# End of a row of gated tiles in a hybrid decoder trunk: the order of the last row, the next weights' split and the forms

## What is computed

```python
def swiglu(x, wi, wo):
    g, u = jnp.split(x @ wi, 2, axis=-1)
    return (jax.nn.silu(g) * u) @ wo

def ffn_half(x, g_pre, g_post, wi, wo):
    return x + 0.5 * rmsnorm(swiglu(rmsnorm(x, g_pre), wi, wo), g_post)
```

## Time and profile before

| what | value |
|---|---|
| time of the kernel, median of 3 runs (lowest to highest) | 2131.16 us (2128.97 to 2131.18) |
| time of the profiled execution itself | 2131.25 us |
| span of the profile, first to last instruction | 2129.5 us |
| TensorE busy | 2045.5 us, 96% |
| VectorE, ScalarE, GpSimd busy | 1385.2, 799.4, 299.6 us |
| mean granted TensorE clock | 0.986 of full speed |
| HBM traffic over the span | 93 GB/s |

### The profile page before, as it was taken

How to read it: one execution, slowest core, us unless ns; L and a number is a source line. 1 busy time by engine, 2 the same in 40 slices (tenths; PEclk the granted TensorE clock), 3 DMA queues, 4 the chain that set the end, 5 groups by cost and what they waited for, 6 DMA issues and landing times.

```text
span 2129.5 us, 38394 instructions
## 1 busy us (share of the span) xinstructions
PE 2045.5 (96%) x16696; PEld 2015.8 (95%) x16696; DVE 1385.2 (65%) x1963; ACT 799.4 (38%) x1053; POOL 299.6 (14%) x293
## 2 busy tenths in 40 slices
PE   8999899999999989899999999998998998999899
PEld 8899899999999989899999999998998998999898
DVE  6756365856768746456687656474987873746567
ACT  5423133423354413233444323232485441423243
POOL 1022040032200004032000031230000001303100
PEclk9999999999999999999999999999999999999999
DMA  4222232144422223223222222222222212323222
GB/s 162 82 88 86 87 105 100 65 155 152 157 72 80 77 77 108 87 90 116 94 80 79 92 94 95 92 85 80 87 95 80 100 68 76 106 90 100 100 90 80
DMA packets 69960, 202.83 MB, mean 95 GB/s; under 512 B 6144, under 2 KB 40224, under 8 KB 60320
## 3 DMA queue, kind: packets, MB, share of 16 engines
q1 hardware_dynamic: 64368, 183.88, 25.0%
q0 software_dynamic: 5424, 16.50, 2.4%
HBM read 193.78 MB, written 4.48 MB: 93 GB/s over the span
## 4 chain that ended last, share of the span: by engine, by line
PE 67%; DVE 17%; ACT 6%; DMA 6%; issue 4%; POOL 1%; DVEq 0%; ACTq 0%; SPq 0%
PE acc L2102 26%; PE acc L2283 14%; PE acc L2272 13%; PE acc L2212 9%; DMA raw<-in_weights 6%; DVE w_lo L1273 3%; ACT w_hi L824 3%; DVE t L1386 2%; PE acc L2143 1%; DVE x L1393 1%; DVE act_lo L1399 1%; DVE rs_post L1381 1%; DVE y L1554 1%; DVE form_lo L1573 1%; PE acc L2341 1%
## 5 line engine op out<-in xcount | busy, mean ns | idle before, releaser
L1273 DVE TENSOR_TENSOR w_lo<-raw,w_hi 128x1024 fp32r<-128x1024 f32 (+3 forms) x245 | 454.6, 1856 | 171.8 <-ACT w_hi L824 171.7
L824 ACT ACTIVATE w_hi<-raw 128x1024 fp32r<-128x1024 f32 (+3 forms) x245 | 373.7, 1546 | 415.7 <-DMA raw<-in_weights 273.4
L2283 PE MATMUL acc<-act_hi,w_hi 128*128 128x260 f32 x1056 | 298.6, 283 | 1.8 <-DVE act_lo L1573 1.8
L2283 PE MATMUL acc<-act_lo,w_hi 128*128 128x260 f32 x1056 | 298.2, 282 | 0.0
L2283 PE MATMUL acc<-act_hi,w_lo 128*128 128x260 f32 x1056 | 298.1, 282 | 0.0
L674 POOL TENSOR_TENSOR raw<-raw 128x512 f32<-128x512 f32 x66 | 124.4, 1884 | 1184.0 <-DMA raw<-in_weights 1184.0
L2102 PE MATMUL acc<-hid_hi,w_hi 128*128 128x260 f32 x1024 | 213.4, 290 | 48.4 <-DVE hid_lo L1626 47.0
L2102 PEld LDWEIGHTS acc<-hid_hi,w_hi 128*128 128x128 f32 x1024 | 163.2, 195 | 51.3 <-DVE hid_lo L1626 49.5
L2102 PE MATMUL acc<-hid_lo,w_hi 128*128 128x260 f32 x1024 | 211.0, 288 | 0.0
L2102 PE MATMUL acc<-hid_hi,w_lo 128*128 128x260 f32 x1024 | 210.9, 288 | 0.0
L2283 PEld LDWEIGHTS acc<-act_hi,w_hi 128*128 128x128 f32 x1056 | 199.3, 189 | 3.4 <-DVE act_lo L1573 3.2
(11 more groups left out here) (353 smaller groups left out, 4113.0 us busy)
## 6 DMA issues: line engine op xcount, KB each, us to landing
raw<-in_weights SPq DMA_DIRECT2D x72, 1024.0 KB, 4.8
raw<-in_weights SPq DMA_DIRECT2D x136, 512.0 KB, 3.7
raw<-in_weights SPq DMA_DIRECT2D x32, 896.0 KB, 4.5
ring<-in_k_pages POOLq DMA_DIRECT2D x16, 256.0 KB, 3.7
raw<-in_weights SPq DMA_DIRECT2D x12, 256.0 KB, 5.0
x<-in_x SPq DMA_DIRECT2D x8, 260.0 KB, 6.3
out_y<-x SPq DMA_DIRECT2D x8, 260.0 KB, 2.0
ckb<-ch_rows POOLq DMA_DIRECT2D x8, 256.0 KB, 4.7
```

The costliest lines, as they stand in the source:

```text
L824: nc.scalar.activation(w_hi[n][:, at:size], raw(n, size)[:, at:size], ACT.Copy).then_inc(hi_ready, 1)
L1273: nc.vector.tensor_tensor(w_lo[n][:, at:size], raw(n, size)[:, at:size], w_hi[n][:, at:size].bitcast(F32), ALU.subtract).then_inc(lo_ready, 1)
L2283: ins = nc.tensor.matmul(out, w[n + 1][:, at:at + P], cols(part[:, c, :], half), start=bool(start) and c == 0 and k == 0, stop=c == 3 and ...
```

## The change

In words:

- Row ends. In sum_hidden the split of unit n + 1 (ACT and DVE) stays only where unit n is a `sums` unit, that is, not for the last pair of a phase. There it moves behind sum_hid_hi on ACT and behind sum_low on DVE.
- The split of the first `plain` unit of a sub-layer is due after job g of the last plain pair and no longer after u. On ACT its place is the same (after the Silu); on DVE it goes between the drains of g and u.
- Forms. stream, differences, first_low and ACT's forms run one pair sooner. difference_lows and block_lows keep their place.
- Recurrent block. On DVE conv_gates(2) goes ahead of the split due at xr4, conv_gates(6) ahead of the drain of gt2, scan(1) ahead of the drain of gt4, scan(3) ahead of the split due at gt4, mixed(4) and mixed(5) ahead of the drain of gt7.
- Head. The DMAs of the gains and of chunk 0 of x are issued by ACT and no longer by SP. ACT runs one Copy on a single column before its first wait for data. TensorE runs 14 matmuls of 128 columns in full fp32 on a constant tile before its first job.

The diff, with what repeats these words left out:

```diff
+WARM = 14
...
                     pl.last_of_sums[f"{s}.plain{j}"] = f"{s}.d{j}"
+                    if j == FIRST_SUM(s):
+                        pl.early[pl.unit[f"{s}.plain{j}"]] = f"{s}.g{j - 1}"
...
-                    if i == 0 and n == 0:
-                        sp.dma_start(params[:, gains], params_d[:, gains]).then_inc(in_gains, 16)
                     c = 2 * i + n
-                    sp.dma_start(x[:, c, :], x_d[:, c, :]).then_inc(in_x[c], 16)
+                    if c:
+                        sp.dma_start(x[:, c, :], x_d[:, c, :]).then_inc(in_x[c], 16)
...
+            act.dma_start(params[:, gains], params_d[:, gains]).then_inc(in_gains, 16)
+            act.dma_start(x[:, 0, :], x_d[:, 0, :]).then_inc(in_x[0], 16)
             act.wait_ge(consts_made, 3)
+            nc.scalar.activation(table_use[:, :], eps[:, :], ACT.Copy).then_inc(table_set, 1)
...
                 nc.scalar.activation(g, g, ACT.Silu).then_inc(silu_ready, 1)
+                done(f"{s}.g{j}")
                 if s or j:
                     done(f"{s}.u{j}")
...
                 split(n)
-                split(n + 1)
+                if is_sums(n):
+                    split(n + 1)
                 wait_drained(act, f"{s}.c{j}")
...
-                        if j == FIRST_SUM(s) - 3:
+                        if j == FIRST_SUM(s) - 4:
                             forms(s, 0, 1)
-                        if j == FIRST_SUM(s) - 2:
+                        if j == FIRST_SUM(s) - 3:
                             forms(s, 1, 6)
                     sum_hid_hi(s, b - 1)
+                    split(U[f"{s}.plain{b - 1}"] + 2)
...
                     scaled(g, f"{s}.g{j}")
+                    done(f"{s}.g{j}")
                     scaled(up, f"{s}.u{j}")
...
-                split_low(n + 1)
+                if is_sums(n):
+                    split_low(n + 1)
...
-                begun = FIRST_SUM(s) - 4
+                begun = FIRST_SUM(s) - 5
                 prepare = {begun: [lambda: stream(s, range(0, 4))], begun + 1: [lambda: stream(s, range(4, KC))],
                            begun + 2: [lambda: differences(s), lambda: first_low(s)],
-                           begun + 3: []}
+                           begun + 3: [lambda: difference_lows(s), lambda: block_lows(s)]}
...
                     sum_low(s, b - 1)
+                    split_low(U[f"{s}.plain{b - 1}"] + 2)
...
             pe.wait_ge(consts_made, 3)
+            for _ in range(WARM):
+                nc.tensor.matmul(acc[ACCS - 1][:, 1, 0:P], mean_of[:, :], mean_of[:, :], start=True, stop=True)
```

More of the change, by code:

```diff
@@ L428, in par @@
             return params[0:parts, at:at + n]
+        gains = slice(*(PARAMS["norm"][0] + i for i in (0, DEPTH * NN * KC)))
         def gain(s, which, c, scaled=False):
@@ L624, in _ @@
         def _(sp):
-            gains = slice(*(PARAMS["norm"][0] + i for i in (0, DEPTH * NN * KC)))
             for i in range(4):
@@ L1010, in out_squares @@
                     done(f"{s}.out{m}")
-                if POSTS.index(s + 1):
-                    act.wait_ge(table_set, POSTS.index(s + 1))
+                act.wait_ge(table_set, POSTS.index(s + 1) + 1)
                 nc.scalar.activation(table_use[:, :], eps[:, :], ACT.Sqrt).then_inc(table_set, 1)
@@ L1026, in ffn @@
                         hidden(s, j)
+                        if j == FIRST_SUM(s) - 4:
+                            forms(s, 0, 1)
                         if j == FIRST_SUM(s) - 3:
-                            forms(s, 0, 1)
-                        if j == FIRST_SUM(s) - 2:
                             forms(s, 1, 6)
                     sum_hid_hi(s, b - 1)
+                    split(U[f"{s}.plain{b - 1}"] + 2)
                     if b < FT:
@@ L1713, in ffn @@
                             continue
-                        if j == begun + 3:
-                            difference_lows(s)
-                            block_lows(s)
                         hidden(s, j)
@@ L2003, in recurrent @@
                 conv_lo(1)
+                conv_gates(s, 2)
                 done(f"{s}.xr4")
-                conv_gates(s, 2)
                 gates(0)
@@ L2021, in recurrent @@
                 done(f"{s}.i3")
+                conv_gates(s, 6)
                 last_drain(gt, "gt", 2)
-                conv_gates(s, 6)
                 done(f"{s}.gt2")
@@ L2031, in recurrent @@
                 scan(0)
+                scan(1)
                 last_drain(gt, "gt", 4)
                 conv_lo(7)
-                scan(1)
                 scan(2)
+                scan(3)
                 done(f"{s}.gt4")
@@ L2038, in recurrent @@
                 last_drain(gt, "gt", 5)
-                scan(3)
                 decode_rows(0, 4)
@@ L2054, in recurrent @@
                 decode_rows(4, 6)
-                last_drain(gt, "gt", 7)
                 mixed(4)
                 mixed(5)
+                last_drain(gt, "gt", 7)
                 mixed_lo(4)
```

## The result

The changed kernel takes **2064.56 us** (median of 4 runs, 2062.69 to 2065.66) against 2131.17 us for the kernel before (4 runs): a ratio of 0.9688, 95% interval 0.9671 to 0.9705. The gain is 66.6 us; 67.8 were forecast. The profiled execution took 2063.59 us, its span 2061.9.

The account below looks back on a forecast made before the run. TensorE, busy 2045.5 of 2129.5 us, was taken as the bound; row ends 47.0, clock 13.0, forms 4.0, recurrent block 2.0 and head 1.8 sum to 67.8 us, giving 2063 us, range 2055 to 2081.

Parts of the forecast that it names:

- Row ends, 47.0: At twelve row ends TensorE's waits for the last gated row's low part (hid_lo) all vanish: 47.0 us.
- The rival of the late unit: Second next unit's split comes late, TensorE waits 2 us at six row ends: 2081 us in all; chance 0.10.
- The clock, 13.0: Without the six long row-end waits TensorE's clock has no reason to fall behind them: 13.0 us.
- Forms, 4.0: Forms made a pair sooner, less the early split's cost: 4 us in all, bounds a 2.5 loss and 5.2 + 3.0 gain.
- the net 0.8 each: Forms in s = 2, 6 and 0: low forms 1.4 us earlier, less u's later drain of 0.7, net 0.8 each.
- I took 1.9: Forms in s = 4: moved work fills DVE's wait for TensorE before a split, 1.9 us with shorter waits around it.
- Recurrent block, 2.0: DVE's new order brings two products 2.2 us earlier, TensorE's first wait at line 2341 vanishes: 2.0 us, bounds 0 and 4.1.
- Head, 1.8: Start of the kernel: table load ahead of the data and 14 warming matmuls gain 1.8 us, bounds -0.5 and 3.2.
- the 1.28 of the table load: In the head, ACT's table load moves ahead of the data: 1.28 us, the sure part of the head's gain.
- The 3.1: In the head, the 14 fp32 matmuls take about 3.1 us at half the clock, over before the data.
- ACT's chunk by chunk work paces this stretch: In the head, ACT sets the pace of the first 18 matmuls, so beyond 1.28 us the gain is only partial.
- The slower rival: TensorE working without rest lowers its granted clock over the span; at 4 points the time is 2145 us; chance 0.04.

Follow-up runs that it names:

- experiment 3: Kernel before, with 48 extra matmuls of overwritten result ahead of each of the six long waits; 2114.34 us against 2130.09, ratio 0.9927.
- experiment 5: Changed kernel with the gains and chunk 0 of x issued by SP as before; mean of squares begins at 23.93 us against 23.62.
- experiment 4: Changed kernel without the 14 fp32 matmuls (WARM = 0); mean of squares begins at 25.25 us against 23.62.

## Why the prediction was right

- *Row ends, 47.0.* Right in the steps too: at the end of the earlier trace rows 2.94 us against 2.95 for the last row, 8.45 against 8.5 for the moved split, and no wait for hid_lo at any of the twelve. The rival of the late unit fell with that: what was spare stayed spare, and the two waits of 0.7 before line 2110 are what s = 2 showed before the change too.
- *The clock, 13.0.* Right in mechanism, shown by filling the waits. The size may be some us too small, but this is not proven: 15.7 in experiment 3 has an interval of 12.1 to 19.2, and the 17.3 us of busy time that the row ends alone saved are the difference of two single profiles. How many stretches at the lower clock lie elsewhere differs between executions: the kernel before has 0.79 from 72 to 80 and from 1640 to 1648, experiment 3 has 1.00 there. Row ends and clock together measure 62.6 for 60.0.
- *Forms, 4.0: the term that was off.* For s = 2 and 6 the net 0.8 each is 0.85 (55.54 to 54.68, 55.53 to 54.70), and by the two parts forecast: the forms sooner give 1.5 (forecast 1.4), the early split takes 0.6. For s = 4 I took 1.9 and charged no early split; there the forms sooner give 0.1 (109.99 to 109.92), the early split takes 0.6 (109.32 without it), and against the kernel before 0.5 is lost. The moved work does not just fill DVE's idle time. DVE's timeline of the changed kernel there:

```profile
1125.02 1.78 DVE L1554 TENSOR_TENSOR gu<-gu 128x520 f32<-128x520 f32 x1
1127.58 1.19 DVE L1557 TENSOR_TENSOR hid_lo<-gu,hid_hi 128x520 fp32r<-128x520 f32 x1 [0.78 <-ACT hid_hi L958]
...
1135.05 2.03 DVE L1281 TENSOR_TENSOR w_lo<-raw,w_hi 128x1792 fp32r<-128x1792 f32 x1 [1.69 <-ACT w_hi L827]
...
1146.23 5.28 DVE L1582 TENSOR_TENSOR act_lo<-y,act_hi 128x520 fp32r<-128x520 f32 x5
```

and POOL's:

```profile
1123.31 2.93 POOL L677 TENSOR_TENSOR raw<-raw 128x512 f32<-128x512 f32 x1 [98.85 <-DMA raw<-in_weights]
1126.32 1.08 POOL L681 TENSOR_TENSOR raw<-raw 128x256 f32<-128x256 f32 x1
...
1146.53 1.53 POOL L677 TENSOR_TENSOR raw<-raw 128x512 f32<-128x512 f32 x1 [18.31 <-DMA raw<-in_weights]
```

  Where DVE waited 1.62 us for TensorE before this split, it now waits 1.69 for ACT. The product lies beside POOL's sums, for 1.78 us, where it took 0.69 in the kernel before; hid_lo takes 1.19 (1.37 before, 0.70 alone). And the last five low forms lie beside the next sums as they did before: 5.28 us (5.29 before), 3.13 in s = 2. That is the case for which the forecast named the Trainium skill, SBUF — State Buffer, section "Who interferes with whom": in s = 4 these rows agree with it, in s = 2 and 6 the gain came all the same. That these rows are why the move gives nothing in s = 4 is read from them; no run took the sums away. For s = 0 no gain of 0.8 is seen: the waits for forms there were 1.07 and 2.08 us and are one of 3.02, the longest of all. (The term's lower bound should read 0.6 x 4 = 2.4.) And at the start of a phase of s = 2 and of s = 6 TensorE now waits 1.5 us for w_lo, which it did not before (0.3 in the run of the row ends alone). Without the early split the one of s = 2 is gone, the one of s = 6 isn't; but with it, too, experiment 5 has 0.3 in s = 2 and experiment 4 has 0.3 in s = 6, so what makes them is not settled.
- *Recurrent block, 2.0.* 1.85, with the first of two waits gone and the second as long, as forecast.
- *Head, 1.8.* 0.4 to 0.6 (to 23.62, from 24.02 in the timeline or 24.19 in the chain). The 14 matmuls give 1.5 to 1.6; the 1.28 of the table load, called sure, is not seen, since without them the mean begins 1.06 us later than in the kernel before. The start fell behind, at 7.40 and not near 5.7, since the loads landed later. The matmuls, 5.66 us long where I had 3.1, ended only at 6.85 and would have held a start at 5.7. The 3.1 came of a misreading: the four rows are records of two matmuls (line 2247 has one for each half of the columns), as the 14 are 28 records; with two in place of four the same sum gives 6.1. "ACT's chunk by chunk work paces this stretch" failed for the cold TensorE (experiment 4) and holds for the warm one.
- *The slower rival*, a clock lowered by work without rest, didn't come: 0.998.

The sum: 62.6 for the row ends with their clock leaves 4.0 of the 66.6 for the rest. As the two measurements have intervals of 3.6 us to each side, this remainder is not told from nothing; the terms come from the stretches: 1.85 for the recurrent block, some 0.5 for the head, and 1.2 (0.86 + 0.83 - 0.48, about nothing in s = 0) for the forms less the early split. That the total was so near is partly luck: row ends and clock came out 2.6 higher, forms and head some 4 lower.

## What to carry to other kernels

Where an engine works in program order, look for a step that waits for something late (here a load) standing ahead of one whose data are there: swapping them on both engines concerned won 62.6 us with no instruction more or less. On DVE alone it won 22.3. Price an idle TensorE at its wait plus what the clock takes behind it: here about a quarter of the gain (15.7 us), and filling a wait with spare matmuls gets that quarter alone. A step put ahead of a queue should be one that doesn't itself wait; and effects of 1 to 2 us are judged in the stretch of the trace between two fixed events, not in the total.

## What the runs showed of the hardware beyond that

- A matmul in full fp32 stands in the trace as two records: 14 of 128x128 from a standing start are 28 records and take 5.66 us (5.19 in the run of experiment 5).
- Two DMAs from a second queue (56 and 260 KB), put beside SP's, made the first 256 KB of weights usable 0.86 us later (5.11 against 4.25).
- A wait of TensorE of about 2 us (1.96 and 2.06) had a lowered clock behind it in one execution and not in another of the same kernel; where it had, it cost 1.7 us.
